# The scan of a bidirectional RWKV-7 layer: steps of 64 tokens in place of 128, and the Gram products of both directions in one visit

## What is computed

```python
def step(S, inp):
    r_t, w_t, k_t, v_t, a_t, b_t = inp
    sa = jnp.einsum('bhvk,bhk->bhv', S, a_t)
    S = S * w_t[:, :, None, :] + sa[..., None] * b_t[:, :, None, :] + v_t[..., None] * k_t[:, :, None, :]
    return S, jnp.einsum('bhvk,bhk->bhv', S, r_t)
```

## Time and profile before

| what | us |
|---|---|
| median of three runs | 2692.49 (2692.34 to 2693.08) |
| span of the profiled execution, first to last instruction | 2688.9 |
| PE busy | 2568.6 (96%) |
| DVE busy | 1872.8 (70%) |
| POOL busy | 1188.7 (44%) |
| ACT busy | 1081.2 (40%) |
| mean granted TensorE clock | 0.983 |

### The profile page before, as it was taken

The page is one execution under the profiler, slowest core; times in us unless marked ns, Lnnn a source line. Parts: engine busy times, 40 slices in busy tenths (PEclk is TensorE's granted clock), DMA queues, the critical chain, the costliest instruction groups (busy, mean ns, idle before and its releaser), DMA issues.

```text
span 2688.9 us, 67501 instructions
## 1 busy us (share of the span) xinstructions
PE 2568.6 (96%) x28608; PEld 2413.9 (90%) x28608; DVE 1872.8 (70%) x2978; ACT 1081.2 (40%) x1978; POOL 1188.7 (44%) x1154
## 2 busy tenths in 40 slices
PE   4899999999999998999999998999799999999998
PEld 3899999999999996777777777999799999999998
DVE  3365675856758565787666657799778678677686
ACT  3434243342433422433333333443453453443534
POOL 1323232322323225555555545656446556565662
PEclk8999999999999999999999998999899999999999
DMA  8333425334254364445454456453223332333231
GB/s 325 106 102 118 140 71 186 113 111 140 80 175 123 101 203 116 131 133 149 142 155 139 145 162 181 133 179 98 61 63 86 81 101 63 87 82 100 63 79 71
DMA packets 282409, 329.10 MB, mean 122 GB/s; under 512 B 76288, under 2 KB 215936, under 8 KB 273536
## 3 DMA queue, kind: packets, MB, share of 16 engines
q1 hardware_dynamic: 274448, 278.66, 33.4%
q0 software_dynamic: 5904, 39.32, 6.9%
q10 hardware_dynamic: 1760, 6.82, 0.6%
HBM read 221.83 MB, written 91.36 MB: 116 GB/s over the span
## 4 chain that ended last, share of the span: by engine, by line
PE 85%; DVE 8%; issue 2%; ACT 2%; DMA 2%; SPq 1%; POOL 0%; DVEq 0%; ACTq 0%; POOLq 0%
PE ser L972 18%; PE gbank L972 13%; PE inv L972 11%; PE bank L972 11%; PE gbank L1416 8%; PE inv L1416 8%; PE ser L1416 7%; PE bank L1416 7%; DVE a_sum L2323 1%; DMA ring<-in_wblocks 1%; PE inv L1174 1%; DVE a_sum L2327 1%; PE bank L1157 1%; DVE a_sum L2331 1%; DVE a_lo L2297 1%
## 5 line engine op out<-in xcount | busy, mean ns | idle before, releaser
L954 POOL TENSOR_TENSOR w_lo<-raw_w,w_hi 128x512 fp32r<-128x512 f32 x264 | 427.3, 1632 | 366.9 <-ACT w_hi L1756 366.9
L849 POOL TENSOR_TENSOR wsp<-ring,wsp 128x1024 fp32r<-128x1024 f32 x67 | 205.2, 3063 | 653.9 <-ACT wsp L1518 653.9
L1756 ACT ACTIVATE w_hi<-raw_w 128x512 fp32r<-128x512 f32 x264 | 165.2, 633 | 261.6 <-PE ser L1416 98.4
L972 PE MATMUL ser<-xn_hi,wsp 128*128 128x384 f32 x816 | 217.1, 339 | 6.0 <-POOL xn_lo L855 6.0
L1416 PE MATMUL gbank<-a_hi,w_hi 128*128 128x288 f32 x616 | 185.8, 302 | 30.8 <-POOL w_lo L954 14.6
L972 PE MATMUL gbank<-xn_hi,wsp 128*128 128x384 f32 x800 | 212.6, 339 | 0.3 <-issue 0.3
L972 PE MATMUL bank<-xn_hi,wsp 128*128 128x384 f32 x800 | 210.2, 337 | 0.5 <-issue 0.5
L972 PE MATMUL inv<-xn_hi,wsp 128*128 128x384 f32 x800 | 210.4, 338 | 0.0
L2126 DVE TENSOR_TENSOR gmat<-gbank,gmask 128x1024 f32<-128x1024 f32 x144 | 175.6, 1219 | 43.8 <-PE gbank L972 43.0
L1742 ACT ACTIVATE a_hi<-a_sum 128x1152 fp32r<-128x1152 f32 x88 | 103.0, 1172 | 224.5 <-DVE a_sum L2331 78.6
L972 PE MATMUL gbank<-ub 64*64 64x128 f32 (+1 forms) x3456 | 179.4, 310 | 9.0 <-DVE gmat L2126 7.6
(11 more groups left out here) (402 smaller groups left out, 7541.1 us busy)
## 6 DMA issues: line engine op xcount, KB each, us to landing
ring<-in_wblocks SPq DMA_DIRECT2D x107, 512.0 KB, 5.3
ub<-op_d SPq DMA_DIRECT2D x144, 256.0 KB, 2.8
raw_w<-in_wquads SPq DMA_DIRECT2D x33, 1024.0 KB, 4.8
raw_w<-in_wquads POOLq DMA_DIRECT2D x22, 1024.0 KB, 9.5
op_d<-ar SPq DMA_DIRECT2D x32, 576.0 KB, 5.4
op_d<-bk SPq DMA_DIRECT2D x32, 576.0 KB, 6.2
raw_w<-in_wquads SPq DMA_DIRECT2D x44, 256.0 KB, 3.7
raw_w<-zsum POOLq DMA_DIRECT2D x11, 1024.0 KB, 13.1
```

Of the source, the lines that this page charges most:

```text
L849: GT(wsp[s % 2][1][:], ring[(N_ADA_RING + s) % RING][:], wsp[s % 2][0][:].bitcast(F32), ALU.subtract).then_inc(S["wsplit_lo"], 1)
L954: GT(w_lo[n % 4][:], src, w_hi[n % 4][:].bitcast(F32), ALU.subtract).then_inc(S["wl_ok"], 1)
L972: return nc.tensor.matmul(out, lhsT, rhs, start=start, stop=stop)
L1756: A(w_hi[s][:], raw_of(op)[:, m, :].rearrange("p (k c) -> p k c", k=KH), ACT.Copy).then_inc(S["wh_ok"], 1)
```

## The change

The serial part of a unit now runs in two steps `k` = 0, 1 of 64 tokens (`SC`), forward direction on its chunk's first half and backward on its second half in `k` = 0, and the other way round in `k` = 1. The matrices are 64x64, the inverse needs two levels (`LEVELS` 5) and its last block no longer has an ACT copy of its own; the Gram products between the two halves of a chunk are not made. Each serial group is issued twice a unit with 64x64 matmuls, on quarters of the array: `ur_state`, `ur_out`, `serial_u`, `u_out`, `serial_s`, `states`, `y_state`, `serial_y`. `ur_keys` takes the place of `serial_ur`. `gram(v)` fills one bank pair with both directions and DVE masks both with one instruction. It runs three units ahead instead of four. `carried` goes to ACT, two instructions for each `k`. The masking on POOL takes five instructions a unit in place of nine. The transposes of `token_major` share a bank with the gram products, so that the one waits for the copy of the other. The decay sums of the dense stage are 18 scans of 64 tokens in place of nine of 128. The diff's core:

```diff
+SC = 64
...
-LEVELS = 6
+LEVELS = 5
...
+AHEAD = 3
...
+def sub(d, j, k):
+    return 2 * chunk(d, j) + side(d, k)
...
-        banks += [ctx.enter_context(nc.psum_tensor(f"bank{i}", [P, 512], F32)) for i in range(2, 4)]
+        su = ctx.enter_context(nc.psum_tensor("su", [P, 2, 512], F32))
+        banks += [su[:, 0, :], su[:, 1, :]]
...
+                pool.wait_ge(S["gram_ok"], v + 1)
+                ch.step(GT(ltc[q][:], g[:, 0, :, 0, :], g[:, 1, :, 0, :], ALU.add))
+                ch.settle()
+                for lev in range(FIRST, LEVELS):
+                    GT(lm[v % 2][lev - FIRST][:], ltc[q][:], two(offm[:, lev - FIRST, :]), ALU.mult).then_inc(S["lm_ok"], 1)
...
+                pool.wait_ge(S["xt_ok"], v + 2)
+                GT(tt[v % 2][:], xt[:, place_of(v), :, :].unsqueeze(1).to_broadcast([P, 2, 2, HD]),
+                   ttm[:].unsqueeze(2).to_broadcast([P, 2, 2, HD]), ALU.mult).then_inc(S["tri_ok"], 1)
...
+            def gram_of(u, d, at):
+                for h in range(2):
+                    hs = halves_of[h]
+                    for n, b in enumerate(halves_of):
+                        smm(gbank[halves_of[n ^ h], h, at:at + SC], u[hs, d, 0, b], u[hs, d, 2, b], True)
+                for h in range(2):
+                    hs = halves_of[h]
+                    for b in halves_of:
+                        smm(gbank[b, h, at + SC:at + 2 * SC], u[hs, d, 2, b], u[hs, d, 1, b], True)
+                for h in range(2):
+                    hs = halves_of[h]
+                    for b in halves_of:
+                        ins = smm(gbank[b, h, at + 2 * SC:at + 4 * SC].rearrange("p (a t) -> p a t", t=SC), u[hs, d, 3, b], u[hs, d, 0:2, b], True)
...
+                if there(v + AHEAD - 1):
+                    pe.wait_ge(S["gram_ok"], v + AHEAD)
...
+            def ur_keys(u):
...
+                    pe.wait_ge(S["u_ok"], 2 * u)
+                order = (1, 0) if j == NC_LAT else (0, 1)
+                for k in order:
+                    for d in range(2):
+                        b = halves_of[side(d, k)]
+                        for h in range(2):
+                            ins = smm(su[halves_of[side(d, k) ^ h], h, UR[k]:UR[k] + HD], g[b, d, h, 2, :], vb[q][b, d, halves_of[h]], k == order[0])
+                    if k == 1:
+                        ins.then_inc(S["ak_full"], 1)
+                    elif j == NC_LAT:
+                        ins.then_inc(S["ur_full"], 1)
...
+            def ur_state(u, k):
...
+                for d in range(2):
+                    pe.wait_ge(S["s_ok"], states_before(u, k) - 1 + d)
+                    x = side(d, k)
+                    for h in range(2):
+                        hs = halves_of[h]
+                        ins = smm(su[halves_of[x ^ h], h, UR[k]:UR[k] + HD], ub[q][hs, d, 0, halves_of[x]], state[k][hs, d, :], False)
+                ins.then_inc(S["ur_full"], 1)
...
+            def serial_u(u, k):
...
+            def y_state(u, k):
...
+            def serial_s(u, k):
...
+            def serial_y(u, k):
...
+            for s in range(-AHEAD, UNITS):
...
+                if serial:
+                    ur_keys(s)
                 if inverses:
+                    if round_of(s) == 0:
+                        e, last = FL.emptied(PAIRS - 1, "zb")
+                        pe.wait_ge(ev[e], last)
+                    if serial and j == 4:
+                        modulation_turned(p, s)
                     turn(s)
+                if serial:
+                    ur_state(s, 0)
+                if there(s - 1):
+                    serial_y(s - 1, 1)
+                if ahead:
+                    gram(s + AHEAD)
+                if serial:
+                    serial_u(s, 0)
+                if inverses:
+                    left(s)
+                if serial:
+                    serial_s(s, 0)
+                if serial:
+                    ur_state(s, 1)
+                    y_state(s, 0)
+                for x in finals(s):
+                    mean(*x)
+                if inverses:
+                    pe.wait_ge(S["p1_ok"], round_of(s) + 1)
+                for x in finals(s - 1):
+                    gate(*x)
+                    spread(*x)
+                if inverses:
+                    right(s)
+                if serial:
+                    serial_y(s, 0)
+                    serial_u(s, 1)
+                    y_state(s, 1)
+                if ahead:
+                    pe.wait_ge(S["gram_ok"], s + AHEAD + 1)
+                for x in finals(s):
+                    variance(*x)
                 if there(s + 1):
                     token_major(s + 1)
                 if serial:
...
+                    serial_s(s, 1)
                     if j == 2:
...
+                        modulation(s)
+            serial_y(UNITS - 1, 1)
             for x in finals(UNITS - 1):
+                gate(*x)
...
+            def carried(u, k):
...
+                    c = sub(d, j, k)
+                    A(stg[:, d, :], state[k][:, d, :], ACT.Copy, scale=g[:, p, d, c:c + 1]).then_inc(S["stg_ok"], 1)
             def y_out(u):
...
+            for s in range(-AHEAD, UNITS):
                 p, j = divmod(s, NC)
...
+                if there(s):
+                    ur_out(s, 0)
+                    if j == 3:
+                        act.wait_ge(S["ada_full"], 4 * p + 4)
+                        A(mrow[:], banks[1][:, :], ACT.Copy).then_inc(S["mrow_ok"], 1)
                 if there(s - 1):
                     y_out(s - 1)
...
                 if there(s):
...
+                    u_out(s, 0)
+                    carried(s, 0)
                 if in_flight(s):
                     product_out(s)
                 if there(s):
...
+                    ur_out(s, 1)
+                    carried(s, 1)
                 for x in finals(s):
                     squares_of(*x)
...
+                if there(s):
+                    u_out(s, 1)
...
-                for c in range(NC):
-                    o, x = (cum[:, c * C:(c + 1) * C], lw[:, c * C:(c + 1) * C])
+                for c in range(NS):
+                    o, x = (cum[:, c * SC:(c + 1) * SC], lw[:, c * SC:(c + 1) * SC])
                     if d == 1:
                         o, x = o[:, ::-1], x[:, ::-1]
-                    ch.step(V.tensor_tensor_scan(o, ones[:], x, 0.0, mul, add))
+                    ch.step(V.tensor_tensor_scan(o, ones[:, 0:SC], x, 0.0, mul, add))
                 ch.settle()
...
+            def gram(v):
+                dve.wait_ge(S["gram_full"], v + 1)
+                V.tensor_tensor(gmat[v % SETS][:].rearrange("p d h x t -> p h d (x t)"), gbank[:, :, :].rearrange("p h (d x) -> p h d x", d=2),
+                                gmask[:].unsqueeze(1).to_broadcast([P, 2, 2, 4 * SC]), mul).then_inc(S["gram_ok"], 1)
...
+                if there(s + AHEAD):
+                    gram(s + AHEAD)
                 if NC <= s < NC + SUB - 1:
                     substitution(PAIRS - 1, [s - NC], [0])
...
+                if there(s):
+                    states(s, 0)
+                for x in finals(s):
+                    centred(*x)
+                if in_flight(s):
+                    summed(s)
                 for x in finals(s - 1):
                     scaled(*x)
                 if NC <= s < NC + SUB - 1:
                     substitution(PAIRS - 1, [s - NC], [1])
...
                 if there(s):
...
+                    states(s, 1)
                     if j == NC_LAT and p + 1 < PAIRS:
                         first_state(p + 1)
...
+            y_add(UNITS - 1)
             for x in finals(UNITS - 1):
...
```

More of the change, by code:

```diff
@@ L30 @@
 C = 128
+SC = 64
 NC_LAT = LAT // C
 NC = T // C
+NS = T // SC
 PAIRS = 8
@@ new lines, in smm @@
+            def smm(out, lhsT, rhs, start):
+                return nc.tensor.matmul(out, lhsT, rhs, start=start, stop=True, skip_group_check=True)
+            def gram(v):
+                q = v % LOADS
+                pe.wait_ge(u_in[q], 80 * (v // LOADS + 1))
+                if v:
+                    pe.wait_ge(S["gram_ok"], v)
+                s = v - AHEAD
+                if there(s):
+                    pe.wait_ge(S["tok_ok"], s + 1)
+                    for p, c, n in finals(s - 1):
+                        pe.wait_ge(S["std_ok"], n + 1)
+                    if s % NC == 3:
+                        pe.wait_ge(S["mrow_ok"], s // NC + 1)
+                for d in range(2):
+                    ins = gram_of(ub[q], d, 4 * SC * d)
+                ins.then_inc(S["gram_full"], 1)
@@ L1360, in _ @@
                 if serial:
-                    ur_state(s)
-                if ahead:
-                    gram(s + 4, 0, (0, 1, 2))
-                if serial:
-                    serial_ur(s)
-                    if j == 4:
-                        pe.wait_ge(S["ada_ok"], p + 1)
-                for x in finals(s - 1):
-                    spread(*x)
-                if inverses:
-                    left(s)
-                if serial:
```

(42 more changed lines are left out.)

482 lines of the change are left out of this document (218 added, 264 removed).

## The result

The changed kernel takes 2742.6 us in the median (2738.4 to 2747.0, 4 runs), the kernel before 2692.8 beside it (2692.3 to 2693.6). The ratio is 1.0184, with a 95% interval of 1.0169 to 1.0198: slower by 50 us, where 42 us less were forecast. It lies outside the range.

What follows compares the result with a forecast made beforehand. PE was taken to bound the unit, serial waits hidden. 2692.5 less 36 (scan's units), less 10 (start of the scan), plus 4 (clock) gave 2650.5: forecast 2650 us, own range 2620 to 2690, wider range 2605 to 2725.

Steps and rivals of the forecast that it cites:

- Start of the scan: From the first gram to the first `ur_state`: three steps instead of four, one copy each, two levels; -10 us.
- Dense stage: 144 more scans on DVE, up to 58 us of DVE time, costed at nothing because PE hides them.
- A: Time in a unit from `ur_state(s,0)` to `ur_state(s,1)`, with DVE's gram copy ahead of `states(s,0)`: 3.35 us.
- B: Time from `ur_state(s,1)` to the next unit's `ur_state`: PE work 2.29, shape changes, hand-offs and states; 3.69 us.
- Five changes of shape at 0.12: 0.6: Time lost on PE where the matmuls' shape changes, in the unit's second part: five times 0.12, 0.6 us.
- rival 2: Small matmul groups cost by their number and hand-offs come later: a unit of 7.9 us, 2715 us, slower; chance 0.13.
- Substitution: In units 9 to 23 each substitution half stands before a `states`: 0.84 us a unit, 0.64 in A; 13 us.
- an ordinary unit is then A + B = 7.04: Length of an ordinary scan unit as the sum of its two chain parts, 3.35 and 3.69: said as 7.0 us.
- Clock: PE's work becomes less dense in the new units; a few short falls of the clock were allowed +4 us.
- The rival that it stays low for a third of the scan: Clock at 0.50 for a third of the units, each 4.3 us longer: 2753 us, slower; chance 0.12.
- Its counter-argument, 14 ns a pair: Against small groups costing by number: 16 rows of quarter-array matmuls on PE start within 0.23 us, 14 ns each.
- The signs listed beforehand: Right: paired `ur` copies every 7.0 us, PE share near 0.8, units 9 to 23 near 8; wrong: other idle patterns.

Runs made afterwards that it cites:

- e5: Changed kernel with direction 1's gram products issued behind the first half's state sums and their masked copy behind its states: ratio 1.0086 to the kernel before.
- e1: Changed kernel with each of the 24 gram products a unit issued as two of half the width, same columns and output: ratio 1.0588 to the kernel before.
- e4: Kernel before the change with each of its 24 gram products a unit issued as two of half the width: ratio 1.0202 to the unedited kernel before.
- e11: Changed kernel with 16 unread products of 2 columns a unit on array quarters, where PE waits for the first half's states: ratio 1.0383 to the kernel before.
- e2: Changed kernel with 16 gram products a unit in place of 24, same columns, 32 instructions fewer, output differs: ratio 1.0112 to the kernel before.
- e9: Changed kernel with 16 products over 128 rows in place of 32 over 64 in output and state sums, output differs: ratio 1.0115 to the kernel before.
- e7: Changed kernel with one unread 128 by 128 product of 256 columns where PE waits for the first half's states: ratio 1.0151 to the kernel before.
- e6: Changed kernel with half-array products of gate, variance and mean each made one and five covered waits dropped, same output: ratio 1.0188 to the kernel before.

## Why the prediction was wrong

**Start of the scan**: -10 forecast, -9.0 measured. Right.

**Dense stage**: 0 forecast, and nothing is seen. Right.

**A**: 3.35 forecast, 3.1 to 3.5 in units without a stall. Right, and the copy on VectorE stood in the way as said: e5 moved it, with half of the Gram products, and A fell by 0.7.

**B**: 3.69 forecast, 4.17 measured, mis-sized by 0.5. The term that failed in it is "Five changes of shape at 0.12: 0.6". In unit 50 PE's part of B, from `ur_state(s,1)` to the end of `serial_s(s,1)`, lasts 3.40 us (1470.78 to 1474.18), the work in it was put at 2.29, so 1.1 us go to changes of shape and gaps; the rest, from there to the next `ur_state`, is 0.76 for 0.80 forecast. This is the size that rival 2 gave to small groups (0.45). An unstalled unit is so near 7.5 us rather than 7.0, some 32 us over 72 units. By itself that would have made 2682, still inside the range.

**Substitution**: A is 3.6 to 4.5 us there without a stall, 0.5 to 1.3 above the others' 3.18, for 0.64 forecast. Right in kind, and near in size.

**The step that failed** is the sum itself, "A: ..., B: ..., an ordinary unit is then A + B = 7.04". It took the issue of an instruction as free at any density. The price stood in no term: at 462 instructions a unit the scan needs 128 blocks in place of 112, and they are asked for in bursts faster than they arrive: a unit of 7.5 us goes through its 1.8 blocks at 4.1 us each, and the next one needs about 4.1 us too (medians of 1.9 to its packet's start and 1.0 for it, then at least 1.2 to its first instruction), and up to 7. Forecast scan 548.5, plus 32 for B, plus the 55 us by which the stalls exceed those of before (64.6 less 9.5), is 636; measured is 72 x 8.885 = 640.

This sum is a reading of one trace, not a strict split: in e5 the stalls grew by 25 us and some 17 us of the edit's worth were missing, so a stall can hide a wait and the reverse. But the runs that change mainly the number of instructions (e1, e4, e11 up, e2 down) all moved the time in its direction, by 2.0 to 4.0 us a block, at a clock of 1.00 too. With the change of the unstalled unit taken off, it is 1.3 us a block in e4, 1.9 in e2, 2.5 in e9 and 2.8 to 2.9 in e11 and e1, lost clock included. The price isn't a constant; it was least in e4, where the stream was not late before the edit.

**Clock**: +4 forecast. The lower clock stood for 53 us of the scan, in 12 stretches; before ten of them PE had stopped at a block end for 1.2 to 2.2 us in the last 8 us. Many such stops were followed by no fall (there were 26 of over 1 us). So the clock's loss looks mostly like a consequence of the stalls, which no run shows by itself; e7 puts about 9 us on what a filler can reach, and e4 shows the stalls' cost without any. The rival that it stays low for a third of the scan didn't come. The sum of that rival has a slip (A at the lower clock is 3.35 + 1.51 = 4.86, not 4.7), on which nothing hangs.

**Rival 2** (small groups cost by their number, 2715) was nearest in size and in kind. Its first half, time lost between the groups, is what B shows. The larger part had another mechanism: not the array and not the hand-offs, since e2 gained 19 us with the unstalled unit unchanged and e9 gained 19 with it longer, but the instructions' way to the engine. Its counter-argument, 14 ns a pair, holds inside a block and misses what happens at its end.

The signs listed beforehand came out mixed: two `ur` copies a unit and the gram copy at 1.22 were there and PE's busy share was 0.82, but units 9 to 23 took 9.1 us in the mean (1100.77 to 1236.63 for 15), not 8, and the sign against the forecast, idle without a releaser inside PE's groups, was not on the list.

Still open are what makes a packet start up to 5 us after the entry into a block, and why packet and first use lie 1.2 us apart at least. No version with whole output is faster than the kernel before; the best is e5.

## What to carry to other kernels

Count an engine's instructions, not only its work: divide them by 256, and compare the time that a block lasts with the time that the next one needs to arrive (here about 4.1 us, in the worst case 7). Cutting a product of the whole array into quarters saves area only where a part of it isn't needed, and it lengthens the stream (here 462 instructions a unit for 403), so it pays only while blocks last longer than that. The reverse has a price too: e6 and e9 made the stream shorter with wider products, and each lost array time. When PE stops inside a group that has no wait and the view says "issue", set its instruction count beside the packets of the instruction queue before you reorder anything.

## What the runs showed of the hardware

PE's instructions arrive as DMA packets of 256, each about 1.0 us long. The packet that a block end waits for starts after the block before has been entered, in the changed kernel at all 128 block ends; over the 14 kernels it started before that in 16 of 1781 (up to 0.9 us, in e11 once 1.2 and once 3.3). In 13 of 14 kernels the shortest time from the end of a packet to the first instruction of its block was 1.0 to 1.24 us (in e11 one entry shows 0.24). Halving the data traffic moved the packets' median start by 0.3 us only. Pairs of weight load and matmul on all four quarters of the array start some 14 to 18 ns apart inside a block (16 in 0.23 us, the 48 of the gram group in 0.85); 32 pairs with 2 columns, on two of the quarters alone, took 30 ns each (1301.31 to 1302.27), and products of 128 rows by 64 columns 47.
